# Three unused SBUF pads that move the start addresses of the matmul operands of a float32r kernel

## The reference

```python
def first_block(x, ...):                       # DEPTH = 1
    h = rglru_block(x, ...)                    # x @ w_in, short conv, two gates, linear recurrence, @ w_out
    x = layer_norm(ALPHA * x + h, ...)
    f = hier_moe(x, ...)                       # 4 groups x 8 experts, top 2, silu(x@w1) * (x@w3) @ w2
    return layer_norm(ALPHA * x + f, ...)

def second_block(x, ...):
    for l in range(2):
        x = x + 0.5 * swiglu(rmsnorm(x, g_ffn1[l]), w1_a[l], w3_a[l], w2_a[l])   # width 2816
        p = rmsnorm(x, g_mix[l]) @ w_in[l]
        merged = gates[:, :, 0] * fourier_mix(...) + gates[:, :, 1] * short_conv(...) + gates[:, :, 2] * pool_mix(...)
        x = x + merged @ w_o[l]
        x = x + 0.5 * swiglu(rmsnorm(x, g_ffn2[l]), w1_b[l], w3_b[l], w2_b[l])
    return rmsnorm(x, g_final)
```

## Time and profile before

| what | value |
|---|---|
| median of 3 runs | 2986.05 us (2983.17 to 2996.56) |
| the profiled execution's own time | 2988.24 us |
| its span, first to last instruction | 2986.4 us |
| matmul records on PE | 16000, busy 2835.5 us (95%) |
| weight loads on PEld | 16000, busy 2449.8 us (82%) |
| VectorE busy | 2187.5 us (73%) |
| ScalarE busy | 1498.5 us (50%) |
| mean granted TensorE clock | 0.975 |

### The profile page before, as it was taken

One profiled execution on the slowest core, in us unless ns is written; L12 is line 12 of the kernel. 1 busy time (PEld: TensorE's weight loads), 2 busy tenths in 40 slices (PEclk: granted clock), 3 DMA queues, 4 the chain that ended last, 5 costly groups with the idle time before them and its releaser, 6 DMA issues.

```text
span 2986.4 us, 41805 instructions
## 1 busy us (share of the span) xinstructions
PE 2835.5 (95%) x16000; PEld 2449.8 (82%) x16000; DVE 2187.5 (73%) x2917; ACT 1498.5 (50%) x1995; POOL 497.3 (17%) x504
## 2 busy tenths in 40 slices
PE   8995999999958999999999999899999999999997
PEld 6674788888847999888888999799998888889996
DVE  6637899999978777666458776887776665687775
ACT  6823788888845444433335444454443332354443
POOL 3214011111012111110113111121111111121111
PEclk9997999999978999999999999999999999999998
DMA  5152999999945555232335646365543332355551
GB/s 215 50 174 90 349 376 373 374 374 380 375 167 140 158 162 157 94 108 88 98 99 135 180 132 177 105 163 148 171 137 99 100 99 94 99 148 156 160 159 57
DMA packets 170155, 516.25 MB, mean 173 GB/s; under 512 B 21600, under 2 KB 22112, under 8 KB 169696
## 3 DMA queue, kind: packets, MB, share of 16 engines
q1 hardware_dynamic: 130176, 422.38, 39.9%
q0 software_dynamic: 37568, 79.72, 12.6%
q10 hardware_dynamic: 2208, 11.43, 1.0%
HBM read 509.24 MB, written 12.58 MB: 175 GB/s over the span
## 4 chain that ended last, share of the span: by engine, by line
PE 81%; DVE 7%; issue 4%; ACT 3%; DMA 2%; POOL 2%; SPq 0%; DVEq 0%; ACTq 0%; POOLq 0%
PE bank L597 27%; PE bank L595 27%; PE bank L596 27%; DVE w_lo L1658 1%; ACT w_hi L1035 1%; PE bank L601 1%; DMA sums<-in_w_b 1%; DVE ft L2033 0%; DMA raw<-in_rec_in 0%; DMA raw<-in_w_b 0%; DVE xT L2084 0%; DMA raw<-in_w_a 0%; POOL mv L1461 0%; DVE st L1748 0%; DVE rsq L2069 0%
## 5 line engine op out<-in xcount | busy, mean ns | idle before, releaser
L1658 DVE TENSOR_TENSOR w_lo<-raw,w_hi 128x1024 fp32r<-128x1024 f32 (+3 forms) x481 | 593.1, 1250 | 286.6 <-ACT w_hi L1035 279.5
L1035 ACT ACTIVATE w_hi<-raw 128x1024 fp32r<-128x1024 f32 (+1 forms) x491 | 507.7, 1046 | 291.1 <-PE bank L597 284.1
L595 PE MATMUL bank<-xf_hi,w_lo 128*128 128x256 f32 x2112 | 593.2, 281 | 48.5 <-DVE xf_lo L2039 22.0
L597 PE MATMUL bank<-xf_hi,w_hi 128*128 128x256 f32 x2112 | 589.8, 279 | 0.0
L596 PE MATMUL bank<-xf_lo,w_hi 128*128 128x256 f32 x2112 | 589.8, 279 | 0.0
L595 PEld LDWEIGHTS bank<-xf_hi,w_lo 128*128 128x128 f32 x2112 | 401.8, 190 | 54.3 <-issue 23.7
L596 PEld LDWEIGHTS bank<-xf_lo,w_hi 128*128 128x128 f32 x2112 | 402.1, 190 | 2.4 <-issue 1.0
L597 PEld LDWEIGHTS bank<-xf_hi,w_hi 128*128 128x128 f32 x2112 | 401.9, 190 | 0.0
L1658 DVE TENSOR_TENSOR w_lo<-raw_more,w_hi 128x1024 fp32r<-128x1024 f32 x249 | 296.6, 1221 | 50.9 <-ACT w_hi L1035 48.2
L597 PE MATMUL bank<-g_hi,w_hi 128*128 128x512 f32 x832 | 327.5, 394 | 0.0
L596 PE MATMUL bank<-g_lo,w_hi 128*128 128x512 f32 x832 | 325.7, 392 | 0.0
(11 more groups left out here) (336 smaller groups left out, 5206.9 us busy)
## 6 DMA issues: line engine op xcount, KB each, us to landing
raw_more<-in_moe SPq DMA_DIRECT2D x249, 512.0 KB, 6.5
raw<-in_moe SPq DMA_DIRECT2D x135, 512.0 KB, 6.6
raw<-in_w_a SPq DMA_DIRECT2D x77, 512.0 KB, 6.4
raw<-in_w_b SPq DMA_DIRECT2D x76, 512.0 KB, 6.1
raw<-in_w_in SPq DMA_DIRECT2D x73, 512.0 KB, 3.6
sums<-in_w_a POOLq DMA_DIRECT2D x88, 256.0 KB, 4.9
sums<-in_w_b POOLq DMA_DIRECT2D x88, 256.0 KB, 4.9
raw<-in_w_a SPq DMA_DIRECT2D x68, 256.0 KB, 6.1
```

The source lines that it names most:

```text
L595: e.matmul(out, a_lo, b_hi, start=start, stop=False, skip_group_check=partial)
L597: return e.matmul(out, a_hi, b_hi, start=False, stop=stop, skip_group_check=partial)
L1035: e.activation(split_of(k)[0], source_of(k), ACT.Copy).then_inc(s["hi"], 1)
L1658: e.tensor_tensor(lo, source_of(k), hi.bitcast(F32), ALU.subtract).then_inc(s["lo"], 1)
```

## The change

Three tiles that no instruction reads or writes are named at three places, so that everything named behind them starts later: by 384 bytes from `raw` on, by 832 from the first tile behind `ones` on, and by 1248 from `sil` on in the experts' group. The instructions of every engine and their order are the same as before (16710 rows in the TensorE program of either).

```diff
         bank = [ctx.enter_context(nc.psum_tensor(f"bank{i}", [P, 512], F32)) for i in range(8)]
+
+        sb("pad_raw", [P, 96])
         raw = sb("raw", [P, NRAW, W])
         w_hi = sb("w_hi", [P, NSPLIT, W], F32R)
         w_lo = sb("w_lo", [P, NSPLIT, W], F32R)
         params = sb("params", [P, NPAR])
         consts = sb("consts", [P, NCONST])
         ones = sb("ones", [P, P])
+        sb("pad_ones", [P, 112])
...
                 cnt = sb("cnt", [P, 1], U32, moe)
+                sb("pad_router", [P, 104], into=moe)
                 sil = sb("sil", [P, 2, FE], into=moe)
                 hd = sb("hd", [P, 2, FE], into=moe)
                 hT_hi = sb("hT_hi", [P, 2, FE], F32R, moe)
```

## The result

The changed kernel takes 2992.24 us (median of 20 runs, 2990.11 to 2997.56), the kernel before, run beside it, 2987.08 us (20 runs, 2982.95 to 2996.56). The ratio is 1.0017, 95% interval 1.0011 to 1.0023: slower, by 5 us of 2987 and by less than the 0.5% that was taken for no change. The forecast was 3057 us.

A forecast was written before the change was run, and what follows sets the result against it. PE was taken to bound the kernel, with no idle time in the experts or a SwiGLU. Terms of 35.5, 30.6 and 5.3 us summed to 71 us, from 2988.2 to 3059, forecast as 3057 us; 8-in-10 range 2885 to 3075.

The forecast's parts named there:

- What bounds the kernel: In the experts and SwiGLU, PE has no idle time, so each matmul step's change lands in the span one for one.
- Reading A: Float32r operand pairs: reads starting at the same place of a 512-byte period collide, 6.6 ns per matmul; 3057 us, chance 0.47.
- B: Every float32r matmul: each operand starting off a larger boundary costs 6.6 ns; faster, 2872 or 2957 us, chance 0.38.
- The term `w`/`xf`, 35.5 us: 6336 matmuls of 256 columns go from 114.4 to 120 ns a step, 35.5 us slower.
- The term of the wide streams, 30.6 us: About 5376 matmuls of 512 columns, `w` by `g`, `xg`, `pc`, `x`, go from 229.7 to 235.4 ns, 30.6 us slower.
- The bound below: For the 512-column streams of `w`: at least the trace's worst wide step, 233.3 ns, 19 us slower.
- The term `xeT`, `hT` and `x`, 5.3 us: 2544 matmuls with these stationary and `w` moving go from 233.3 to 235.4 ns, 5.3 us slower, bounded below by 0.
- DMA in the experts' stage: DMA engines busy 0.98 of the time, so PE could be only about 2% faster there before they bind.
- No change: Matmul steps: set by something no start address moves, `e` slow for another reason; 2986 us, chance 0.15.
- The states flip: Two steps at equal addresses fall differently: all fast saves 6 + 5 us, all slow costs 41 us; not a case.
- the direction: Whole kernel: slower by more than 0.5%, 15 us, given chance 0.47.

The follow-up runs named there:

- The streams alone: A kernel without the computation, running only 36-matmul streams at chosen operand starts, other engines idle: 120.0 and 113.1 ns at 256 columns, 227.2 and 233.4 at 512.
- the third run: Changed kernel with two more pads, `xf` at 64 and `e` at 0, wide streams still at difference 0: 2976.25 us, ratio 0.9961.
- the best version: Changed kernel with `g`, `xf` and `e` at 64, but `xg`, `pc` and the experts' tiles at 0: 2964.91 us, ratio 0.9928 to the kernel before.
- the fifth run: A kernel of streams without the computation, each behind another stream or a wait: 256 columns at difference -64 step at 113.1 or 118.0 ns.

## Why the prediction was right or wrong

- **What bounds the kernel.** Right. PE has no idle time in either stage, and each step lands in the span: the steps' net of +3 us stands beside +4.3 us of span.
- **Reading A against B.** Right in what decides, wrong in how. The streams alone and the first pad alone show that a pair moved together keeps its step, so it is how two starts stand to each other, as A has it. But A says that two reads "that start at the same place of a 512-byte period get in each other's way, once per matmul, for 6.6 ns". At 512 columns the same place is the fastest of all, and at 256 columns 160 bytes apart costs as much as 0 (119.8 ns). The period is 256 bytes and not 512, which changes nothing here.
- **The term `w`/`xf`, 35.5 us.** Right: 6336 x 5.6 ns = 35.5 us by the steps alone, +33.3 with the waits taken in, and +31 by that count where it was made alone. The forms came as said, 120 ns in every stretch and `e` and `w` alike.
- **The term of the wide streams, 30.6 us ("With one surcharge 228.8 + 6.6 = 235.4").** This step failed, in size and in sign. A surcharge of 6.6 ns, read off a pair of 256 columns, was added to a step of 512. Measured were 226.7 to 227.5 ns: -14.4 us instead of +30.6. The bound below was wrong with it: it took 233.3 as the least that a difference of 0 could cost and left out a gain. What the runs put in its place is a loss that is 32 cycles at a difference of 0 at 256, 384 and 512 columns alike, while the other differences' loss is larger at the larger width: 16 to 32 cycles at 256 columns, 37 to 50 at 512. One pair of one width could not show that.
- **The term `xeT`, `hT` and `x`, 5.3 us.** The same step, again with the wrong sign: -16.8 us. Taking this pad away costs 17 us.
- **DMA in the experts' stage ("only about 2% faster there before they bind").** Too low, or no limit at all. The sixteen transposes of `hd` in this stage lie from 312.4 to 837.0 us before and from 310.5 to 820.5 after, 34.97 and 34.00 us a pair, 2.8% faster. The DMA share is 0.99 and PE still has no idle time.
- **No change.** The measured time lies in this case, which had 0.15, but not for its reason: it has a step "that no start address moves", and every stream's step but that of `e` moved.
- **The states flip.** Named, sized at +41 to -11 us and left out of the cases. In the changed kernel the two steps of `w`/`xf` and of `w`/`xg` are gone, with the difference of -64 that had them. But in the third run it was the whole miss (31 us), and it is what the best version rests on.

In sum 35.5 + 30.6 + 5.3 = 71 us were forecast and 33.3 - 14.4 - 16.8 = +2 were measured on the same streams. That the pair decides was found and the first term sized; how the cost goes with the width was not. That the direction is right is luck: the first term is by a few us the larger of two that cancel.

## What to carry to other kernels

In a stream of float32r matmuls the starts of the two operands are a tuning knob, and what counts most is their difference modulo 256 bytes: 0 for 512 columns, and for 256 columns neither 0 nor 160 but, for example, -64, so streams that share a tile have to be weighed against each other. Change one stream at a time and read its step from the start times, since a sum near zero can be two large effects. And don't carry a cost per matmul from one width to another: measure it at both, in a kernel that does nothing else, and in more than one order, since a stream can inherit its step.

## What the runs showed of the hardware

- The step of a float32r stream depends on the difference of its operands' starts, with TensorE alone at work: 113.3 to 120 ns for 256 columns, 226.6 to 234.3 for 512, 173.3 to 176.8 for 384; 128 columns take 111.7 at any difference. Why 32 cycles at a difference of 0, and which part of the chip they are spent in, no run shows.
- The page "SBUF — State Buffer" of the Trainium skill, section "Who interferes with whom", has the moving operand's port and the weight load's independent. The runs don't fit this as far as two operands' starts alone change the step by 6 to 7 ns a matmul with all else idle; where in the chip they meet is open.
- The page "TensorE: Matmul & The Clock Gate" of the Trainium skill, section "Back-to-back issue gap", gives 109.2 and 215.8 ns for the isolated gap of a matmul of 256 and 512 columns. No float32r stream here comes nearer than 113.3 and 226.6; the plain float32 matmuls do, with some 215 ns for each of their two passes.
- At the difference of -64 a 256-column stream has two steps, 113.3 and 117.8 ns, and which one it gets is mostly inherited from the stream ahead. A wait of half a microsecond or a wide stream of difference 0 ends the fast one; a narrow stream of difference 0 starts it (five times of five in the fifth run, 37 of 40 in the kernel before). At +64 both steps were seen too, but there a narrow stream of difference 0 didn't start the fast one, the one time it was tried.
